# Gate and up projections that walk their 512 columns in pieces from either half, on one Trainium2 core

## The reference, cut to what matters

```python
D_MODEL = 2048
D_FF = -(-8 * D_MODEL // (3 * 256)) * 256        # 5632

def _swiglu(u, w_gu, w_down):                    # u 256x2048, w_gu 2048x11264, w_down 5632x2048
    gate, up = jnp.split(u @ w_gu, 2, axis=-1)
    return (jax.nn.silu(gate) * up) @ w_down
...
    for layer in range(DEPTH):                   # DEPTH = 2
        ...
        u = rmsnorm(h, norm_g[layer, 2])
        h = h + rmsnorm(_swiglu(u, ffn_w_gu[layer], ffn_w_down[layer]), norm_g[layer, 3])
```

## Time and profile before

| what | value |
| --- | --- |
| median of 3 runs | 2815.58 us (2814.97 to 2816.5) |
| the profiled execution: span from first to last instruction | 2812.7 us |
| its own time | not listed apart from its span; the median is 2.9 us above the span |
| PE busy | 2787.0 us, 99% of the span |
| weight loads of PE busy | 2320.3 us, 82% |
| DVE busy | 1578.5 us, 56% |
| ACT busy | 1368.8 us, 49% |
| mean granted TensorE clock | 0.999 of full speed |
| DMA | 481.12 MB, 171 GB/s over the span |

### The profile page before, as it was taken

How to read it: one execution, slowest core, us unless ns; L and a number is a source line. 1 busy time by engine, 2 the same in 40 slices (tenths; PEclk the granted TensorE clock), 3 DMA queues, 4 the chain that set the end, 5 groups by cost and what they waited for, 6 DMA issues and landing times.

```text
span 2812.7 us, 33205 instructions
## 1 busy us (share of the span) xinstructions
PE 2787.0 (99%) x13548; PEld 2320.3 (82%) x13548; DVE 1578.5 (56%) x2212; ACT 1368.8 (49%) x2031; POOL 61.0 (2%) x83
## 2 busy tenths in 40 slices
PE   9999999999999999999999999999999999999998
PEld 7788888888888888888888888888888888887777
DVE  6665777755545454444644555654555544466666
ACT  6645454545444444333634544644444443356565
POOL 0000000000000000000010000000000000000002
PEclk9999999999999999999999999999999999999999
DMA  7855544665666666555655434666666655565444
GB/s 233 139 128 131 108 105 99 167 208 178 193 182 193 189 190 190 188 194 187 218 172 155 135 105 153 191 189 193 187 190 185 194 188 191 190 204 170 153 142 135
DMA packets 213497, 481.12 MB, mean 171 GB/s; under 512 B 15584, under 2 KB 16352, under 8 KB 212704
## 3 DMA queue, kind: packets, MB, share of 16 engines
q1 hardware_dynamic: 210848, 467.78, 56.9%
q0 software_dynamic: 2352, 11.17, 1.1%
q10 hardware_dynamic: 144, 0.05, 0.0%
HBM read 476.84 MB, written 2.10 MB: 170 GB/s over the span
## 4 chain that ended last, share of the span: by engine, by line
PE 90%; DVE 5%; ACT 2%; DMA 1%; issue 1%; POOL 0%; SPq 0%; ACTq 0%; POOLq 0%
PE PS L1105 19%; PE PS L1107 19%; PE PS L1106 19%; PE PS L1154 8%; PE PS L1153 8%; PE PS L1152 8%; DVE WL L2150 1%; DVE WORK L2309 1%; PE PS L1366 1%; ACT WH L1628 1%; PE PS L1269 1%; PE PS L1486 1%; PE PS L1184 1%; PE PS L1281 1%; PE PS L1282 1%
## 5 line engine op out<-in xcount | busy, mean ns | idle before, releaser
L2150 DVE TENSOR_TENSOR WL<-RAW,WH 128x1024 fp32r<-128x1024 f32 x826 | 1011.0, 1225 | 940.8 <-ACT WH L1628 939.1
L1628 ACT ACTIVATE WH<-RAW 128x1024 fp32r<-128x1024 f32 x830 | 874.8, 1055 | 841.6 <-PE PS L1107 526.9
L1105 PE MATMUL PS<-WH,UTH 128*128 128x512 f32 x2396 | 955.9, 399 | 3.9 <-DVE WL L2150 3.0
L1107 PE MATMUL PS<-WH,UTL 128*128 128x512 f32 x2396 | 935.1, 390 | 0.0
L1106 PE MATMUL PS<-WL,UTH 128*128 128x512 f32 x2396 | 934.0, 390 | 0.0
L1105 PEld LDWEIGHTS PS<-WH,UTH 128*128 128x128 f32 x2396 | 450.2, 188 | 99.3 <-issue 4.0
L1107 PEld LDWEIGHTS PS<-WH,UTL 128*128 128x128 f32 x2396 | 449.8, 188 | 97.3
L1106 PEld LDWEIGHTS PS<-WL,UTH 128*128 128x128 f32 x2396 | 450.6, 188 | 87.1
L1154 PE MATMUL PS<-WH,HTL 128*128 128x512 f32 x656 | 259.3, 395 | 0.0
L1153 PE MATMUL PS<-WL,HTH 128*128 128x512 f32 x656 | 258.8, 394 | 0.0
L1152 PE MATMUL PS<-WH,HTH 128*128 128x512 f32 x656 | 255.4, 389 | 0.0
(11 more groups left out here) (421 smaller groups left out, 2413.4 us busy)
## 6 DMA issues: line engine op xcount, KB each, us to landing
RAW<-in_ffn_w_gu SPq DMA_DIRECT2D x352, 512.0 KB, 4.3
RAW<-in_ffn_w_down SPq DMA_DIRECT2D x176, 512.0 KB, 4.5
RAW<-in_ab_w_in SPq DMA_DIRECT2D x128, 512.0 KB, 4.7
RAW<-in_nsa_w_in SPq DMA_DIRECT2D x80, 512.0 KB, 3.7
RAW<-in_w_in SPq DMA_DIRECT2D x64, 512.0 KB, 4.0
RAW<-in_ab_w_out SPq DMA_DIRECT2D x32, 512.0 KB, 4.6
RAW<-in_nsa_w_out SPq DMA_DIRECT2D x32, 512.0 KB, 4.2
RAW<-in_w_out SPq DMA_DIRECT2D x16, 512.0 KB, 4.4
```

The costliest lines, as they stand in the source:

```text
L1105: e.matmul(o, lh, wh[:, j], start=k + j == 0, stop=False)
L1107: x = e.matmul(o, ll, wh[:, j], start=False, stop=k + j == NKT - 1)
L1628: e.activation(wh, raw, ACTF.Copy).then_inc(*a_hi.inc(s))
L2150: e.tensor_tensor(wl, raw, wh.bitcast(F32), ALU.subtract).then_inc(*v_lo.inc(s))
```

## The change

`woven` reorders the 512 columns of the bank and of both moving operands in the same way, in stage 1 with pieces of 16 columns and in stage 3 with pieces of 8. Piece 0 is columns 0 to 15 (0 to 7), the next is columns 256 to 271 (256 to 263), then 16 to 31, then 272 to 287, and so on. A matmul of stage 1 then walks 32 pieces and one of stage 3 walks 64. Each result column is made of the same products and lands at the same place. All other stages keep their contiguous walk, and no other engine has any edit.

```diff
                         o = banks.ap("acc", st, c, t)[:, 0:wd]
                         lh, ll = UTH[:, k + j, 128 * t:128 * t + 128], UTL[:, k + j, 128 * t:128 * t + 128]
-                        e.matmul(o, lh, wh[:, j], start=k + j == 0, stop=False)
-                        e.matmul(o, lh, wl[:, j], start=False, stop=False)
-                        x = e.matmul(o, ll, wh[:, j], start=False, stop=k + j == NKT - 1)
+                        o, hi, lo = (woven(x, st) for x in (o, wh[:, j], wl[:, j]))
+                        e.matmul(o, lh, hi, start=k + j == 0, stop=False)
+                        e.matmul(o, lh, lo, start=False, stop=False)
+                        x = e.matmul(o, ll, hi, start=False, stop=k + j == NKT - 1)
                 x.then_inc(*(p_mm.inc(s) if 1 in ts else p_mm.inc("t0", s)))
+
+            def woven(x, st):
+
+                piece = {1: 16, 3: 8}.get(st)
+                return x.rearrange("p (a b c) -> p b a c", a=2, c=piece) if piece else x
```

## The result

The changed kernel takes 2875.91 us (median of 4 runs, 2875.13 to 2882.33) against 2815.7 us before: the ratio is 1.0213, with a 95% interval from 1.0197 to 1.0228. It is 60 us slower. The forecast was no change, and the range ended at 2867 us, 9 us short.

The account below looks back on a forecast made before the run. TensorE was taken as the bound, so time is matmuls times distance between starts; longer descriptions, jumps and a vanishing stall summed 0 + 0 + 0 on the 2812.7 us span, median 2.9 us above: 2815.6 us, range 2783 to 2867.

Parts of the forecast that it names:

- no change: Whole kernel: the time stays at 2815.6 us, with a range of its own of 2810 to 2821; chance 0.43.
- What bounds the kernel: Gate/up stages: TensorE is busy 99% of the span, so a changed distance between matmul starts reaches the end one for one.
- (a): Instructions of the gate/up matmuls: longer operand descriptions are taken in while the matmul before runs; put at 0.
- (b): Jumps between pieces, reading operands or writing the bank, stages 1 and 3: 0 to 0.25 ns each, up to 51 us; taken as 0.
- The 0.25 ns of the range's end: Price per jump from 60 scattered columns, 290 ns against 275 contiguous: 17 us in stage 1, 34 us in stage 3.
- VectorE's free jumps: On VectorE piece length didn't change the time; taken to say that reading in pieces is not dear in itself.
- rival 1: Stages 1 and 3: each piece costs, stage 3 raised twice as much; 51 us at 0.25 ns, 2866 us; chance 0.35.
- The rule of the Trainium skill: PSUM lines are 8 bytes, non-contiguous access slows matmuls much, two neighbours should be contiguous; no figure given.
- (c): Contiguous walk of gate/up matmuls: a stall may go away, at most 7 ns each, 30 us; taken as 0.
- The split of the 13 ns: Time above the clock per 512-column matmul: 7 ns go with the columns, some 6 ns are there whatever its length.
- the first test named: Profile after, stages 1 and 3: 16 matmul starts in a row should again be 3.62 us apart.

Follow-up runs that it names:

- e1_read: Changed kernel with only the moving operands read in pieces (16 columns in stage 1, 8 in stage 3), bank contiguous: 2874.68 us, 1.0212 of the kernel before.
- e2_write: Changed kernel with only the bank written in pieces, moving operands read contiguously: 2815.04 us, 1.0001 of the kernel before.
- e7_tile: Kernel before with stationary tiles of fewer columns, other starts or steps per pair of chunks; only distances used: 32 columns, contiguous walk, 231.7 ns against 227 plain.
- e10_16x8: Kernel before with stage 1 in pieces of 8 columns from 16 places, stage 3 of 4 from 32 and terms outermost: 2808.73 us, 0.9975.

## Why the prediction was wrong, point by point

- **What bounds the kernel**: right. TensorE alone, and a change of the distance went to the end one for one (61 us of distances, 60.9 us of span).
- **(a), the longer descriptions**: right at 0; with them in every gate/up matmul, writing alone moved nothing.
- **(b), the jump between pieces**: this step failed, in "Between 0 and 0.25 ns I take 0". A walk in pieces costs where it is read: the distance rose by 12.7 ns with 32 pieces and by 16.1 ns with 64, which would be 0.40 and 0.25 ns per jump. The 0.25 ns of the range's end gave 17 us in stage 1 and 34 us in stage 3; 27 and 34 us were measured. So stage 3 stands where the range ended, and the 9 us by which it was too short are all in stage 1, because the price is not in proportion to the number of pieces. That 0.25 came out right for 64 pieces is luck: it was made of a duration of 290 against 275 ns on line 1406, whose 60 columns lie all apart, in a matmul of the full fp32 type with starts 113 ns apart. And VectorE's free jumps were given weight for an engine that reads more than twice as fast; they say nothing on TensorE.
- **The form of the price**: wrong also in rival 1, which had it per jump, "twice as many jumps in stage 3", with stage 3 raised twice as much. It was raised by a quarter more. Its direction was right; it left open whether the operand or the bank pays, which e1_read and e2_write decided. Its 0.35 was too low: the argument that no slack hides anything spoke for it, and for a narrow "no change".
- **The rule of the Trainium skill** ("Advanced Engine Details and Errata", section Memory Cachelines) on PSUM patterns that are not contiguous: for this case the runs say no. The bank written in pieces of 8 and 16 kept 226.7 ns and the time within 0.1%; in pieces of 4 only together with the moving operand, never dearer for it than the reading alone. The page's other half, two neighbours at a time, was kept by every run and so isn't tested.
- **(c), a stall that goes away**: nothing was gained by this change. The split of the 13 ns into 7 that go with the columns and 6 that don't was weaker than it looked: the 256-column row has 32 stationary columns, and 32 of them alone move the 512-column distance from 226.7 to 231.7 ns (e7_tile). And "evenly 0.22 to 0.23 us" was no ground to think that no order of addresses could avoid the 13 ns above the clock: 4 columns from 32 places and 8 from 16 go below the contiguous walk and down to 220 ns.
- **What would show it**: the first test named, 16 starts in 3.62 us, was the one that decided; it came out at 3.84 and 3.90 us.

Open: why pieces are dear to read at all and by which rule, for example why 2 places cost more than 4 with 8, 16 and 32 columns and less with 4 columns, why 16 columns every 32 cost 240.0 ns again, what the contiguous walk's 13 ns are, and what sets the two rhythms. No run explains these; the tables give their sizes.

## What to carry to other kernels

Where TensorE is busy all the time, the order in which the moving operand is read has a price of its own: keep pieces whole in 16 bytes and start them there (pieces of 16 that start 2 columns off cost 60 ns more, 240 to 300), and don't alternate between two places in pieces under 64 columns. Other numbers of places go from 220 to 278 ns with pieces of 4 and 8 and follow no rule found here, so take them from a run. The order in which the bank is written, in pieces of 8 and 16, was free. Count the matmuls first: at 4224 of them 1.3 ns each is all that separates "no change" from a visible one, so an unknown cost per matmul deserves a wide range or a run, not a 0. One kernel can try eleven patterns in one run if the pairs of chunks each take another, since the trace gives the distances of each.

## What had not been expected of the hardware

- Distances keep to 226.7, 240.0 and 243.3 ns over hundreds of matmuls, whatever ScalarE and VectorE do beside them. That points to TensorE's own reads; no run took the other engines away.
- The contiguous walk minds where it starts, by 4 to 8 ns, and minds it against the place of the stationary tile; moving both by 32 columns (128 bytes) gives 227.3 ns back, moving both by 8 doesn't.
- The same addresses give two stable distances, 221 and 230 ns, that hold for a pair of chunks (190 matmuls) or longer and turn only at transposes (e10_16x8).
- A walk in small pieces can be faster than the contiguous one: the whole kernel in 2790.94 us, 0.9915 of the time before.
